# The head of a hybrid diffusion step reordered: where the first loads are issued, and one projection out of the split scheme

## What is computed

```python
def _adaln(cond, w, b):                       # w_ada: 1024 x 3072 per layer
    m = silu(cond) @ w + b
    return split(m[:, None, :], 3, axis=-1)   # shift, scale, gate

def _layer(x, mods, lp, ...):
    shift, scale, gate = mods
    h = _rmsnorm(x, lp['norm_g']) * (1.0 + scale) + shift
    z = h @ lp['w_in']
    conv_in, conv_gate, ssm_in, ssm_gate, q, k, v, attn_gate, merge = split(z, ...)
    # inside the convolution branch: a, g = split(conv_in, 2); y = a * sigmoid(g); ...
    # the state space branch: lam_bar = exp(lam*dt); b_bar = ((lam_bar-1)/lam) * (b_re + i b_im)
    #   bu = einsum(u, b_bar), a scan over the tokens, then a product with c_re + i c_im
    # attention branch, then the three branches are merged, projected and added to x
```

## Time and profile before

| | before |
|---|---|
| median of 3 runs | 848.39 us (846.63 to 848.56) |
| span of the profiled execution, first to last instruction | 845.0 us |
| busy PE / DVE / ACT / POOL | 712.7 / 605.8 / 316.0 / 172.6 us |
| DMA queue of SP (q1): packets, MB | 78460, 116.52 |
| DMA queue of ACT (q10): packets, MB | 832, 0.53 |
| mean DMA rate over the span | 139 GB/s |

### The profile page before, as it was taken

The page is one execution under the profiler, slowest core; times in us unless marked ns, Lnnn a source line. Parts: engine busy times, 40 slices in busy tenths (PEclk is TensorE's granted clock), DMA queues, the critical chain, the costliest instruction groups (busy, mean ns, idle before and its releaser), DMA issues.

```text
span 845.0 us, 9392 instructions
## 1 busy us (share of the span) xinstructions
PE 712.7 (84%) x3294; PEld 469.8 (56%) x3294; DVE 605.8 (72%) x1103; ACT 316.0 (37%) x563; POOL 172.6 (20%) x121
## 2 busy tenths in 40 slices
PE   4957899990779994988999999999907698999996
PEld 1145665550721533776778558655507456787785
DVE  3378689997355589768866554899973568888664
ACT  1244451111323322454655355401213433545552
POOL 1067449202000009033000100492020000000000
PEclk9979999995789997999999999999967698999999
DMA  6864335350067471554565475454220034555661
GB/s 208 282 146 118 125 128 173 110 145 28 3 155 232 141 239 61 150 150 146 154 184 168 147 236 165 137 166 118 73 99 1 26 99 124 176 174 155 195 177 55
DMA packets 79339, 117.64 MB, mean 139 GB/s; under 512 B 27437, under 2 KB 31869, under 8 KB 79293
## 3 DMA queue, kind: packets, MB, share of 16 engines
q1 hardware_dynamic: 78460, 116.52, 45.6%
q10 hardware_dynamic: 832, 0.53, 0.3%
HBM read 112.51 MB, written 1.38 MB: 135 GB/s over the span
## 4 chain that ended last, share of the span: by engine, by line
PE 52%; DVE 36%; ACT 3%; DMA 3%; issue 2%; SPq 2%; POOL 1%; DVEq 0%; ACTq 0%; POOLq 0%
PE proj L1032 11%; PE proj L1034 10%; PE proj L1033 10%; DVE H L1358 8%; PE proj L730 8%; DVE cvacc L1423 7%; DVE qkt L1358 7%; PE side L765 4%; PE proj L756 3%; DVE qM_split L1358 3%; PE side L963 2%; DVE wide_split L1358 2%; DMA raw<-in_w_ada 2%; DVE H L1575 2%; DVE gates_split L1358 2%
## 5 line engine op out<-in xcount | busy, mean ns | idle before, releaser
L756 PE MATMUL proj<-raw,hT 128*128 128x512 f32 (+1 forms) x320 | 125.1, 551 | 0.0
L1423 DVE SCALAR_TENSOR_TENSOR cvacc<-cvpad,taps,cvacc 128x256 f32<-128x256 f32 x240 | 123.1, 541 | 0.0
L1358 DVE TENSOR_TENSOR wide_split<-raw,wide_split 128x512 fp32r<-128x512 f32 x118 | 90.6, 773 | 41.4 <-ACT wide_split L1086 40.3
L1086 ACT ACTIVATE wide_split<-raw 128x512 fp32r<-128x512 f32 x118 | 74.4, 632 | 95.9 <-PE proj L1034 95.9
L756 PEld LDWEIGHTS proj<-raw,hT 128*128 128x128 f32 x320 | 60.3, 190 | 60.4 <-issue 58.4
L730 PE MATMUL proj<-raw,cond 128*2 128x512 f32 x192 | 88.8, 617 | 5.9 <-DMA raw<-in_w_ada 5.9
L1358 DVE TENSOR_TENSOR H<-H,qkt 128x128 f32<-128x128 f32 x128 | 75.5, 590 | 1.2
L1032 PE MATMUL proj<-wide_split,H_split 128*128 128x512 f32 x154 | 65.0, 422 | 13.2 <-DVE wide_split L1358 12.7
L1783 POOL TENSOR_SCALAR st<-st 128x1 f32<-128x1 f32 (+1 forms) x12 | 3.9, 324 | 336.9 <-DVE st L1692 148.7
L961 PE MATMUL side<-qM,Uz 128*64 128x64 f32 x128 | 20.5, 248 | 54.3 <-DVE HY L1676 54.3
L1033 PE MATMUL proj<-wide_split,H_split 128*128 128x512 f32 x154 | 62.8, 408 | 0.0
(11 more groups left out here) (235 smaller groups left out, 1491.1 us busy)
## 6 DMA issues: line engine op xcount, KB each, us to landing
raw<-in_w_in SPq DMA_DIRECT2D x104, 512.0 KB, 3.8
raw<-in_w_ada SPq DMA_DIRECT2D x48, 512.0 KB, 4.5
raw<-in_w_out SPq DMA_DIRECT2D x16, 512.0 KB, 4.2
raw<-in_w_ssm_glu SPq DMA_DIRECT2D x8, 512.0 KB, 5.2
raw<-in_w_ssm_out SPq DMA_DIRECT2D x8, 512.0 KB, 3.8
raw<-in_w_attn_out SPq DMA_DIRECT2D x8, 512.0 KB, 4.1
raw<-in_w_conv_out SPq DMA_DIRECT2D x8, 512.0 KB, 3.9
raw<-in_w_in SPq DMA_DIRECT2D x8, 256.0 KB, 2.8
```

The source lines that it names most:

```text
L756: m = T.matmul(proj.bank((l, u, s))[:, 0:n], lhs[:, s, kt, :], w[:, i, :], start=(kt == 0), stop=last)
L1086: S.activation(chunk_parts(m)[0], chunk_raw(m), ACT.Copy).then_inc(chunk_hi, 1)
L1358: return V.tensor_tensor(out, a, b, op)
L1423: m = V.scalar_tensor_tensor(acc, src, taps[:, t, j:j + 1], acc, ALU.mult, ALU.add)
```

## The change

- SP issues the first four `w_ada` slabs first, then the C loads, x and the rotary table. The 15 small loads move to ACT's queue, at the head of ACT's program; among them `ldt` now stands third of the seven.
- The B loads of layer 0 move on SP from behind (ada,0,1) to behind the slabs of cg.
- The stage cT of layer 0 moves ahead of (ada,0,1), on PE and ACT.
- cg leaves EARLY in both layers: it is computed as plain fp32 from hT, and waits for the four evictions of hT. The first split chunks made ahead of it are now those of ssm; the split of hT stays, now first needed by ssm.
- The stage hT is divided in two names, hTt (PE's transposes) and hT (the evictions). The order on each engine is as it was.

```diff
-EARLY = ("cg", "ssm", "ca")
+EARLY = ("ssm", "ca")
...
-    return ([("hT", 0), ("hT", 1), ("early", 0), ("early", 1), ("chunks", "cg")]
+    return ([("hTt", 0), ("hT", 0), ("hTt", 1), ("hT", 1), ("early", 0), ("early", 1), ("chunks", "ssm")]
...
     out = [(0, s) for s in (("cond",), ("small", 0), ("tab", 0), ("taps", 0), ("ada", 0, 0), ("xn", 0, 0), ("xn", 0, 1),
-                            ("ada", 0, 1), ("adaT", 0, 0), ("adaT", 0, 1), ("cT", 0), ("preP", 0, 0))]
+                            ("cT", 0), ("ada", 0, 1), ("adaT", 0, 0), ("adaT", 0, 1), ("preP", 0, 0))]
...
@@ SP
-            sp.dma_start(ident[:, :], C["ident"]).then_inc(consts_in, 16)
...
-            small_loads(0)
-            sp.dma_start(expo[:, :], C["expo"]).then_inc(expo_in, 16)
             first = RAW
             for n in range(first):
                 slab(n)
+            c_loads(0)
             sp.dma_start(x[:, 0, :], A["x_prompt"][0]).then_inc(x_in, 16)
...
-                if stg == ("ada", 0, 1):
-                    c_loads(0)
+                if stg == ("unit", "cg") and l == 0:
                     b_loads(0)
@@ PE
+                        if u == "cg":
+                            for s in range(NS):
+                                for h in range(2):
+                                    side.drained(pe, ("hT", l, s, h))
+                            lhs = hT
-                        if u in EARLY:
+                        elif u in EARLY:
@@ ACT
+            act.dma_start(ident[:, :], C["ident"]).then_inc(consts_in, 16)
...
+            small_loads(act, 0)
+            act.dma_start(expo[:, :], C["expo"]).then_inc(expo_in, 16)
...
-                    if stg[1] == "cg":
-                        high_parts(ahead(l, "cg"))
-                        if l:
-                            side.filled(act, ("adaT", l, 2))
+                    if stg[1] == "cg" and l:
+                        side.filled(act, ("adaT", l, 2))
@@ DVE
-                elif k == "unit" and stg[1] in ("cg", "ssm"):
-                    low_parts(ahead(l, stg[1]))
+                elif k == "unit" and stg[1] == "ssm":
+                    low_parts(ahead(l, "ssm"))
```

More of the change, by code:

```diff
@@ L165, in side_uses @@
         return [(("E", stage[1], 4 * stage[2] + i), 1) for i in range(4)]
-    if k == "hT":
+    if k == "hTt":
         return [(("hT", l, stage[1], h), 1) for h in range(2)]
@@ L574, in toeplitz, with small_loads @@
                     eng.dma_start(Mf[rows_, s0, :], KTs[2 * GC:3 * GC, 0, a, :]).then_inc(m_in, 16)
+        def small_loads(queue, l):
+            queue.dma_start(a32[0:G, 0, :].rearrange("g (d p) -> g d p", d=2),
+                            A["ssm_a_re"][l].rearrange("d g p -> g d p")).then_inc(small_in, 16)
+            queue.dma_start(a32[0:G, 1, :].rearrange("g (d p) -> g d p", d=2),
+                            A["ssm_a_im"][l].rearrange("d g p -> g d p")).then_inc(small_in, 16)
+            queue.dma_start(ldt[0:G, :], A["ssm_log_dt"][l].rearrange("d g -> g d"),
+                            allow_slow_non_contiguous=True).then_inc(small_in, 16)
+            queue.dma_start(a32[0:G, 3, :].rearrange("g (d p) -> g d p", d=2),
+                            A["state_ssm_re"][0, l].rearrange("d g p -> g d p")).then_inc(small_in, 16)
+            queue.dma_start(a32[0:G, 4, :].rearrange("g (d p) -> g d p", d=2),
+                            A["state_ssm_im"][0, l].rearrange("d g p -> g d p")).then_inc(small_in, 16)
+            queue.dma_start(taprow[0:TAPS, :], A["conv_dw_w"][l]).then_inc(small_in, 16)
+            queue.dma_start(taprow[TAPS:TAPS + 1, :], A["conv_dw_b"][l:l + 1, :]).then_inc(small_in, 16)
         block = ctx.enter_context(nc.Block())
@@ L580, in _ @@
         def _(sp):
-            def small_loads(l):
-                if l:
[L583 to L595, removed]
             def c_loads(l):
@@ L689, in _ @@
                         results(l)
-                        small_loads(l + 1)
+                        sp.wait_ge(out_done, 64 * (l + 1))
+                        side.filled(sp, ("taps", l))
+                        small_loads(sp, l + 1)
                         unpack_y(l)
@@ L826, in _ @@
                             m.then_inc(side.full, 1)
-                elif k == "hT":
+                elif k == "hTt":
                     s = stg[1]
@@ L1058, in _ @@
             n_chain = [0]
+            act.dma_start(ident[:, :], C["ident"]).then_inc(consts_in, 16)
+            act.dma_start(condrow[0:DT, :], A["c_ctx"].rearrange("(t p) -> t p", p=P)).then_inc(consts_in, 16)
+            act.dma_start(condrow[DT:2 * DT, :], A["c"][0].rearrange("(t p) -> t p", p=P)).then_inc(consts_in, 16)
+            for l in range(DEPTH):
+                act.dma_start(modrow[32 * l:32 * l + 24, :],
+                              A["b_ada"][l].rearrange("(t p) -> t p", p=P)).then_inc(consts_in, 16)
+                act.dma_start(modrow[32 * l + 24:32 * l + 32, :],
+                              A["norm_g"][l].rearrange("(t p) -> t p", p=P)).then_inc(consts_in, 16)
+            small_loads(act, 0)
+            act.dma_start(expo[:, :], C["expo"]).then_inc(expo_in, 16)
             def link(ins):
```

## The result

| | before | after |
|---|---|---|
| median (runs) | 847.51 us (4) | 853.77 us (4) |
| range of the runs | 846.03 to 848.56 us | 852.26 to 855.71 us |
| ratio after/before, 95% interval | | 1.0087 (1.0059 to 1.0115) |
| span of the profiled execution | 845.0 us | 850.5 us |
| busy PE / DVE / ACT / POOL | 712.7 / 605.8 / 316.0 / 172.6 us | 714.5 / 583.7 / 307.5 / 169.4 us |

The change makes the kernel slower: 6.3 us between the medians, 7.4 us by the ratio (5.0 to 9.7). The profiled execution of after took 852.26 us, 1.8 us more than its span; so of the 3.4 us that stand ahead between span and median of before, some 1.6 us are a difference between executions. DVE has 22 us less to do and PE about as much as before, so the loss is in waits. The chain of work that ended last names them. Columns: start us, us, what.

The account below looks back on a forecast made before the run. Layer 0 was bound by PE's ada matmuls, then DVE's splits, with POOL 2.1 us short; layer 1 by PE around cg. Terms +0.9 - 1.0 + 0.6 + 2.4 = +2.9 on 848.4 gave 851.3 us, range 846.0 to 856.5.

Parts of the forecast that it names:

- The start of the ada phase: Layer 0, first ada matmul: small loads land later beside other traffic, +1.0 us, bounds 2.2 earlier and 6.1 later.
- small loads stuck behind slabs: Rival, chance 0.15: small loads land 6.1 us later instead of 1.0, first ada matmul past 15 us, 856.4 us.
- The ada phase itself: Layer 0 ada matmuls: a stall before the last slab goes, -1.0 us, and cT's transposes come in, +0.9 us.
- E': End of layer 0's ada matmuls after the change, forecast 0.9 us later than before.
- E: End of layer 0's ada matmuls in the kernel before, 42.72 us.
- cg in layer 0: Plain cg on PE starts at E' + 6.6, takes 14.00 us, done at E' + 20.6: PE gains 11 us.
- POOL: Layer 0 preP: starts at E' + 9.0, half 0 takes 21.9 us, preE at E' + 30.9; net -1.0 us.
- B and POOL as slow as before: Rival, chance 0.15: B issue 7.0 us and contended POOL, start past E' + 10, preE at E' + 34.9; 855.3 us.
- POOL freed entirely: Rival, chance 0.05: without DVE's splits half 0 of preP takes 17.4 us, preE at E' + 26.4; 846.8 us.
- ssm and ca: Layer 0 behind preE: slow clock after PE's gap, one more chunk split ahead; +0.6 us, bounds -1.0 and +1.2.
- cg in layer 1: PE is the bound there: plain cg makes cg to ssm 14.45 us against 12.08, +2.4 us, bounds +2.2 and +2.5.

## Why the prediction was right, and where it was not

The sign and the place were right: slower, 853.8 us where 851.3 were forecast, with PE idle for 9 us ahead of preE and a 2.4 us loss in layer 1. The size was not: a change of +2.9 us was forecast, and +6.3 (medians) or +7.4 (ratio, 5.0 to 9.7) was measured. Step by step:

- **The start of the ada phase: failed in its size.** I took +1.0 us for the small loads; it was 17.24 - 12.46 = +4.8. The landing grew by 4.0 us, and 0.7 us come from the later issue (6.56 us, 5.83 before), which I had put at nothing. The rival "small loads stuck behind slabs", which was to decide where the first ada matmul comes past 15 us, came in kind: it priced a landing 6.1 us longer and named the slabs, which are the smaller part. I had counted the flow beside the loads in slabs, the only thing that the earlier trace rows showed; the held loads show that slabs alone cost 1.2 us, near the +1.0, and that the C loads and x bring the rest. The C loads and x were in the list of what I named, and I priced nothing for them.
- **The ada phase itself: 1.0 us off.** From the first matmul to E' it takes 48.42 - 17.24 = 31.2 us, before 42.72 - 12.46 = 30.3: +0.9, where the forecast was -1.0 + 0.9 = -0.1. cT took 34.59 - 33.56 = 1.0 us, about as forecast. The stall ahead of the last slab is gone, but it was worth only the 0.44 us that PE itself was idle in the earlier trace rows; I had read 1.0 us off the weight loads. And the first ada matmuls run at half their later rate, for 1 us longer than before (the last section), which costs half of that. With the late start this makes E' = E + 5.7.
- **cg in layer 0: right in that it was early, not in how early.** It starts at E' + 7.0 (6.6 forecast) and takes 15.67 us for 14.00, so PE gained 9.2 us and not 11. It was still done 9 us before POOL, so the slow records at its front lie in front of a wait and cost nothing.
- **POOL: right in its mechanism, 1.3 us off in its start.** First operation E' + 10.3 where I took 9.0, near the bound of 10.4; B's issue took 7.0 us as in layer 0 before, not the 4.6 us of layer 1. Half 0 took 21.4 us for the 21.9 I took. preE came at E' + 31.7, forecast 30.9. So the net of cg and POOL was -0.2 us instead of -1.0. The mark of the rival "B and POOL as slow as before" (a start past E' + 10) was met, but only that half of it came: with an uncontended POOL preE was 3.2 us ahead of the E' + 34.9 that the rival priced.
- **POOL freed entirely: did not happen.** POOL's products took 2.02 us with DVE idle and its sums 2.34; half 0 can't come under about 20.6 us by such rows, and the rival had 17.4.
- **ssm and ca: right in kind, too small.** The clock behind the wait was low, as the windows below show: +1.4 us from the first preE to the second (31.66 us, 30.30 before), forecast +0.6, and 0.2 past the bound of +1.2. The transposes of preE alone took 1.7 us more (3.68 us, 1.99 before).
- **cg in layer 1: right.** 14.51 us from cg to ssm, forecast 14.65 less 0.2 for an earlier start; +2.4 us. ACT's wait for the second ssm slab added nothing.

Columns of the windows: stretch, its us, busy us of PE, PEld, DVE, ACT, POOL, PEclk, DMA share, GB/s. The wait at preE and what follows it, in after:

```profile
71.10:80.17 9.07, 0.02 (x1) 0.00 (x1) 0.20 (x1) 0.60 (x1) 8.78 (x4) 0.63 0.37 116
80.17:84.50 4.33, 4.33 (x20) 4.19 (x21) 0.00 (x0) 2.39 (x4) 0.51 (x1) 0.59 0.00 0
84.50:99.20 14.70, 10.17 (x40) 6.73 (x38) 12.83 (x6) 4.42 (x7) 14.25 (x7) 1.00 0.25 72
```

In the first row hardly anything but POOL works. In the second PE is back, at a granted clock of 0.59, close to the level of 1.2 GHz, and the 16 transposes take 3.68 us where they take 1.99 without the wait. In the third DVE and POOL are both busy and PE has 4.5 us of idle in 14.7: DVE's splits set the rate.

With the terms as measured (+5.7, -0.2, +1.4, +2.4) the sum is +9.3 us. The four terms that were off all have one sign: 3.8 us at the small loads, 1.0 in the ada phase, 0.8 at POOL and 0.8 in ssm and ca. That 851.3 lies within 2.5 us of the measured median is partly luck: it was counted from a median of 848.39, where the four runs beside the changed kernel have 847.51, and the time moved less than the 9.3 us of the rows, within what the interval allows. The large error is a term of its own and was told apart by putting the small loads back.

## What to carry to other kernels

When a chain of waits names one engine, moving its work off the path pays only up to the next engine that is due at the same place: 8 us freed on PE gave 2.4 to 2.9, until the stage that waited for POOL was moved behind work that was ready, which gave 7.6. A load that starts the whole program belongs ahead of the bulk traffic, and a queue of its own does not protect it; all that still flows beside it is to be counted: here 2 MB of slabs, whose traffic ended 2 us after its issue, cost 1.2 us, and 1.6 MB of C, x and rotary table, which flowed on until 14 us, another 3.3 us. Before a unit is changed in all layers, ask in each layer which engine is the bound there.

## What the runs showed of the chip that I had not expected

- **Landing times of a load of a few bytes** (2 KB of taps) issued at about the same moment: 4.50 us with nothing beside it, 5.71 beside four slabs, 9.04 beside slabs, C loads and x. SP's own issue suffers too: the issue of x took 2.49 us behind the C loads with the slabs in flight, 0.64 us behind the slabs alone in the kernel before, and 0.51 us behind the C loads when the slabs had landed (the kernel with C and x held); that of the second pair of C loads took 2.19 us, and 1.06 us when the slabs had landed.
- **POOL and DVE side by side step in pairs.** A POOL product takes 2.02 us alone and 2.36 beside splits, a sum 2.34 and 2.71, so about 0.35 us more each; a split takes 0.68 us alone and about 2.5 beside POOL. The Trainium skill (SBUF — State Buffer, section SBUF: two separate sides) tells of an exclusive lock that blocks the other engine for a whole instruction. On DVE's side the rows agree with it; POOL pays only half of a split's own length, less than the whole instruction, and there the measurement decides.
- **The first ada matmuls run at half their later rate, at a granted clock of 1.00.** The weight loads show the pace, as each waits for the matmul ahead of it: in after they are 0.85 us apart until 22.31 us and 0.43 us apart from there; in before the slow stretch ends at 16.57 us, 1 us less behind its first matmul. Timeline of the weight loads, then the windows:

```profile
21.46 0.13 PEld L721 LDWEIGHTS proj<-raw,cond 128*2 128x2 f32 x1 [0.72 <-issue]
22.31 0.09 PEld L721 LDWEIGHTS proj<-raw,cond 128*2 128x2 f32 x1 [0.72 <-issue]
22.74 0.09 PEld L721 LDWEIGHTS proj<-raw,cond 128*2 128x2 f32 x1 [0.34 <-issue]
```

```profile
17.24:22.30 5.06, 5.06 (x7) 0.73 (x7) 4.36 (x13) 0.23 (x1) 0.00 (x0) 1.00 0.09 11
...
55.40:60.40 5.00, 4.95 (x8) 2.20 (x9) 2.36 (x2) 0.91 (x1) 1.61 (x2) 0.66 0.55 52
```

The second window is the start of plain cg in after, where the granted clock was 0.66 and the unit took 15.67 us. Behind the same idle of 1.7 us the same 32 records took 13.97 us in four of the other kernels. What decides either was not tried.
